# Hybrid attention layer on one core: the bias spread goes memory to memory, weight splits change engine, transposes go inside jobs, and keys are projected two heads at a time

## What is computed

```python
h = rmsnorm(x, g)                                   # 1040 x 1024
(c_q, c_kv, k_r, q_b, k_b, v_b, q_i, k_i, w_i, gate_a, gate_b) = split(h @ w_in)
q_a  = rmsnorm(c_q, g_cq) @ w_uq                    # 8 heads of 64 + 32
kv_a = (rmsnorm(c_kv, g_ckv) @ w_ukv).reshape(B, L, 8, 64 + 64)
k_nope, v_a = kv_a[..., :64], kv_a[..., 64:]
score = einsum('bqh,bqhk->bqk', w_i, relu(einsum('bqhd,bkd->bqhk', q_i, k_i)))
idx = top_k(score, 256)                             # keys of the sparse branch
bias = rel_bias[t5_bucket(idx - pos)]               # 32 buckets x 8 heads
```

## Time and profile before

| | |
|---|---|
| median of 3 runs | 1617.09 us (1616.66 to 1621.89) |
| the profiled execution's own time | 1617.06 us |
| its span | 1615.3 us |
| PE, DVE, ACT, POOL busy | 1400.2, 1035.6, 668.4, 438.2 us |
| index jobs, start of the first and last matmul | 28.0 and 99.9 us |
| first of the 64 steps | 137.2 us |
| first product for the keys of the first branch | 572.6 us |

### The profile page before, as it was taken

How to read it: one execution, slowest core, us unless ns; L and a number is a source line. 1 busy time by engine, 2 the same in 40 slices (tenths; PEclk the granted TensorE clock), 3 DMA queues, 4 the chain that set the end, 5 groups by cost and what they waited for, 6 DMA issues and landing times. The chain is left out here.

```text
span 1615.3 us, 21747 instructions
## 1 busy us (share of the span) xinstructions
PE 1400.2 (87%) x7342; PEld 1132.6 (70%) x7351; DVE 1035.6 (64%) x1946; ACT 668.4 (41%) x1179; POOL 438.2 (27%) x480
## 2 busy tenths in 40 slices
PE   5846999999999998989888988999945999999960
PEld 4645888878989757777666766889944777777730
DVE  4504899999990456666666665443264777777737
ACT  4305722322212146666665654111103666666622
POOL 2202044422212024434543411410002333333213
PEclk9877999999999999999999998999956999999985
DMA  7551031132223000203142205432164999999808
GB/s 205 57 69 40 24 137 53 46 98 82 89 92 110 23 0 5 69 1 99 47 93 60 54 1 190 145 99 79 66 261 147 344 355 356 357 372 376 327 31 324
DMA packets 86750, 217.36 MB, mean 135 GB/s; under 512 B 22712, under 2 KB 47832, under 8 KB 74376
## 3 DMA queue, kind: packets, MB, share of 16 engines
q1 hardware_dynamic: 76296, 195.24, 37.0%
q0 software_dynamic: 9216, 16.80, 2.8%
q10 hardware_dynamic: 1152, 4.19, 0.6%
HBM read 188.27 MB, written 44.70 MB: 144 GB/s over the span
## 5 line engine op out<-in xcount | busy, mean ns | idle before, releaser
L1269 DVE TENSOR_TENSOR pL<-ps,pH 128x512 fp32r<-128x512 f32 (+3 forms) x224 | 127.0, 574 | 113.2 <-ACT pH L1206 112.2
L416 PE MATMUL ps<-hHi,g_lead 128*128 128x512 f32 (+2 forms) x480 | 185.8, 387 | 9.1 <-DVE Qi L844 4.3
L310 DVE TENSOR_SCALAR_CACHE_REDUCE mask<-score,cand 128x272 bf16<-128x272 f32 (+6 forms) x224 | 185.5, 893 | 4.6 <-DVE cand L329 4.4
L417 PE MATMUL ps<-hLo,g_lead 128*128 128x512 f32 (+2 forms) x480 | 185.1, 386 | 0.0
L2178 DVE TENSOR_TENSOR w_rest<-wgu,w_lead 128x1024 fp32r<-128x1024 f32 x128 | 156.0, 1223 | 45.0 <-ACT w_lead L2125 43.8
L418 PE MATMUL ps<-hHi,g_rest 128*128 128x512 f32 (+2 forms) x480 | 184.0, 383 | 0.0
L732 POOL TENSOR_TENSOR g_rest<-g_raw,g_lead 128x2048 fp32r<-128x2048 f32 x16 | 73.6, 4601 | 320.4 <-ACT g_lead L591 320.4
L2125 ACT CAST w_lead<-wgu 128x1024 fp32r<-128x1024 f32 x128 | 134.4, 1055 | 37.9 <-PE ps L2071 37.9
L1206 ACT CAST pH<-ps 128x512 fp32r<-128x512 f32 (+3 forms) x224 | 108.1, 489 | 71.0 <-PE ps L1154 70.1
L2069 PE MATMUL ps<-w_lead,x_lead 128*128 128x512 f32 x256 | 114.1, 446 | 6.0 <-DVE w_rest L2178 6.0
L2091 PE MATMUL ps<-wd,hmT 128*128 128x512 f32 x256 | 115.3, 593 | 1.6 <-DVE hmT L2201 1.0
(11 more groups left out here) (348 smaller groups left out, 3466.3 us busy)
## 6 DMA issues: line engine op xcount, KB each, us to landing
wgu<-in_w_exp_gate SPq DMA_DIRECT2D x32, 1024.0 KB, 7.6
wgu<-in_w_exp_up SPq DMA_DIRECT2D x32, 1024.0 KB, 13.4
wd<-in_w_exp_down SPq DMA_DIRECT2D x32, 1024.0 KB, 13.8
g_raw<-in_w_in SPq DMA_DIRECT2D x16, 1024.0 KB, 5.8
gates_d<-stage SPq DMA_DIRECT2D x32, 256.0 KB, 2.0
gt<-gates_d SPq DMA_DIRECT2D x32, 256.0 KB, 3.2
rel_d<-relf SPq DMA_DIRECT2D x1, 4672.0 KB
KR<-kb_d SPq DMA_DIRECT2D x16, 260.0 KB, 6.4
```

Source lines behind the costliest of these rows:

```text
L310: return dve.tensor_scalar(mask[:, OFF[i]:OFF[i + 1]], score[:, OFF[i]:OFF[i + 1]], thr, 0.0, op, ALU.add, accum_out=cnt[:, i:i + 1])
L416: pe.matmul(dst, x[0], y[0], start=(k == 0), stop=False)
L417: pe.matmul(dst, x[0], y[1], start=False, stop=False)
L1269: dve.tensor_tensor(pL[n % RING][:, lo:512], bank_of(k)[:, lo:512], pH[n % RING][:, lo:512].bitcast(F32), ALU.subtract).then_inc(s_rs, 1)
```

## The change

- SP loads `rel_bias` and `hot` ahead of the first row block; PE makes the bias first, ahead of the row transposes. Row block 3 is loaded ahead of piece 0.
- ACT copies `relf` behind the first square, stores it to a new small `rel_s` (8 x 1168) in memory through its own queue, and behind the index jobs starts the spread from `rel_s` to `rel_d`, memory to memory.
- The remainders of pieces 0 to 3 are made by DVE, at other places of its stream; piece 4 and later stay on POOL. `lead(0)` moves one row block later, so does `lead(1)`; `lead(2)` comes behind all index outputs, `lead(3)` inside the steps.
- The transposes of row blocks 4 to 8 go inside the k loops of index jobs 0 to 2.
- `w_mla_ukv` is loaded as two tiles, `wuk` and `wuv`, with rows of 256 bytes; a key product covers two heads (12 products in place of 24), and both ACT and DVE copy out of each, one head each.

```diff
+        rel_s = dram("rel_s", (H, REL), F32)
-        kv_jobs = [("k", h, n) for h in range(H) for n in range(3)] + [("v", t, 0) for t in range(9)]
+        kv_jobs = [("k", h, n) for h in range(0, H, 2) for n in range(3)] + [("v", t, 0) for t in range(9)]
+
+        def copies(u, n):
+
+            return sum(kind == "k" or m % 2 == u for m, (kind, _, _) in enumerate(kv_jobs[:n + 1]))
...
+                sp.dma_start(rb32[:, :], a["rel_bias"]).then_inc(s_rel, 16)
+                sp.dma_start(hot[:, :], a["hot"]).then_inc(s_rel, 16)
                 rows_in(0)
...
                 rows_in(2)
+                rows_in(3)
                 piece_in(0)
-                rows_in(3)
-                sp.dma_start(rb32[:, :], a["rel_bias"]).then_inc(s_rel, 16)
-                sp.dma_start(hot[:, :], a["hot"]).then_inc(s_rel, 16)
...
-                sp.wait_ge(s_relc, 1)
-                sp.dma_start(rel_d, relf[:, :].unsqueeze(1).to_broadcast([H, P, REL])).then_inc(s_reld, 16)
...
-                            sp.dma_start(wukv[:, :], a["w_mla_ukv"][0]).then_inc(s_uw, 16)
+                            ukv = a["w_mla_ukv"][0].rearrange("c (h n) -> c h n", h=H)
+                            for k, w in enumerate((wuk, wuv)):
+                                sp.dma_start(w[:, :].rearrange("p (h n) -> p h n", h=H),
+                                             ukv[:, :, 64 * k:64 * (k + 1)]).then_inc(s_uw, 16)
...
                     for k in range(KT):
                         mm = three(ps[0:rows_out, 4 + n % 4, 0:hi - lo], (wl[:, k, c], wr_[:, k, c]),
                                    (hHi[:, k, lo:hi], hLo[:, k, lo:hi]), k)
-                    mm.then_inc(s_ij, 1)
+                        if k == KT - 1:
+                            mm.then_inc(s_ij, 1)
+                        if k in rows_between:
+                            transposes(rows_between[k])
...
                 for n in range(len(idx_jobs)):
-                    idx_job(n)
-                    if n < 4:
-                        transposes(4 + n)
-                    if n == 3:
-                        transposes(8)
+                    idx_job(n, {3: 4 + 2 * n, 7: 5 + 2 * n} if n < 2 else {3: 8} if n == 2 else {})
...
-                        if n % 2 == 0:
-                            pe.wait_ge(s_kva, n // 2 - 1)
-                        else:
-                            pe.wait_ge(s_kvd, n // 2 - 1)
+                        pe.wait_ge(s_kva, copies(0, n - 4))
+                        pe.wait_ge(s_kvd, copies(1, n - 4))
...
-                        mm = pe.matmul(bank[0:NOPE, 0:hi - lo], wk[:, i, 0:NOPE], ckvT[:, lo:hi],
+                        mm = pe.matmul(bank[:, 0:hi - lo], wuk[:, 64 * i:64 * (i + 2)], ckvT[:, lo:hi],
                                        start=True, stop=True)
...
+                    if b == 0:
                         act.wait_ge(s_relp, 3)
                         act.copy(relf[:, :], flat[0:H, 4 * 512:4 * 512 + REL]).then_inc(s_relc, 1)
-                    if b == 5:
+                        act.wait_ge(s_relc, 1)
+                        act.dma_start(rel_s, relf[:, :]).then_inc(s_rels, 16)
+                    else:
+                        rows_lead(b - 1)
+                    if b == 3:
+                        lead(0)
+                    if b == 6:
                         lead(1)
...
-                    if n == 7:
-                        lead(2)
-                    if n == 9:
-                        lead(3)
+                lead(2)
+                act.wait_ge(s_rels, 16)
+                act.dma_start(rel_d, rel_s.unsqueeze(1).to_broadcast([H, P, REL])).then_inc(s_reld, 16)
...
+                    if n == 12:
+                        lead(3)
...
-                    if b == 3:
-                        rest(0)
-                    if b == 6:
-                        rest(1)
...
-                for p in range(2, 5):
-                    rest(p)
+                rest(4)
...
+                def rest(p):
+                    dve.wait_ge(s_wh, p + 1)
+                    dve.tensor_tensor(g_rest[p % 2][:, :, :], g_raw[p % 2][:, :, :],
+                                      g_lead[p % 2][:, :, :].bitcast(F32), ALU.subtract).then_inc(s_wl, 1)
...
+                    if b == 7:
+                        rest(1)
                     if b >= 1:
                         rows_rest(b - 1)
+                    if b == 4:
+                        rest(0)
...
+                rest(2)
                 dve.wait_ge(s_wp, 4)
...
                     dve.wait_ge(s_re, n + 1)
+                    if n == 16:
+                        rest(3)
```

More of the change, by code:

```diff
@@ L226, in hybrid_layer @@
         wuq = at("wuq", [P, 2, H * QKD], F32, R_W)
-        wukv = at("wukv", [P, H * 128], F32, R_W + 6144)
+        wuk, wuv = (at(nm, [P, H * 64], F32, R_W + 6144 + off) for nm, off in (("wuk", 0), ("wuv", 2048)))
         qtok = [at(f"qtok{k}", [P, H, QKD], F32, R_W + 10240 + 3072 * k) for k in range(2)]
@@ L288, in step_at @@
             return (1024 * (n % 3) if n < WIDE else 1536 * (n % 2)) + chunks(WID[steps[n][0]])[0]
-        kv_jobs = [("k", h, n) for h in range(H) for n in range(3)] + [("v", t, 0) for t in range(9)]
+        kv_jobs = [("k", h, n) for h in range(0, H, 2) for n in range(3)] + [("v", t, 0) for t in range(9)]
+        def copies(u, n):
+            return sum(kind == "k" or m % 2 == u for m, (kind, _, _) in enumerate(kv_jobs[:n + 1]))
         (s_con, s_gain, s_gb, s_sq, s_nh, s_var, s_rstd, s_xn, s_tr, s_hh, s_hl, s_cb, s_rel, s_relp, s_relc,
-         s_reld) = map(sem, ["s_con", "s_gain", "s_gb", "s_sq", "s_nh", "s_var", "s_rstd", "s_xn", "s_tr", "s_hh",
-                             "s_hl", "s_cb", "s_rel", "s_relp", "s_relc", "s_reld"])
+         s_rels, s_reld) = map(sem, ["s_con", "s_gain", "s_gb", "s_sq", "s_nh", "s_var", "s_rstd", "s_xn", "s_tr", "s_hh",
+                             "s_hl", "s_cb", "s_rel", "s_relp", "s_relc", "s_rels", "s_reld"])
         s_xs = [sem(f"s_x{k}") for k in range(4)]
@@ L418, in three, with idx_job @@
                     return pe.matmul(dst, x[1], y[0], start=False, stop=(k == KT - 1))
-                def idx_job(n):
+                def idx_job(n, rows_between):
                     kind, p, t, part = idx_jobs[n]
@@ L478, in latent_rows @@
                     pe.transpose(ps[0:96, bank, 384:384 + r], krx[b % 2][0:r, :], ident[0:r, 0:r]).then_inc(s_gj, 1)
+                pe.wait_ge(s_rel, 32)
+                for c in range(0, REL, 512):
+                    n = min(512, REL - c)
+                    pe.matmul(flat[0:H, 4 * 512 + c:4 * 512 + c + n], rb32[:, :], hot[:, c:c + n],
+                              start=True, stop=True).then_inc(s_relp, 1)
                 pe.wait_ge(s_con, 16)
@@ L482, in _ @@
                     transposes(b)
[L483 to L489, removed]
-                for n in range(len(idx_jobs)):
-                    idx_job(n)
-                    if n < 4:
-                        transposes(4 + n)
-                    if n == 3:
-                        transposes(8)
+                for n in range(len(idx_jobs)):
+                    idx_job(n, {3: 4 + 2 * n, 7: 5 + 2 * n} if n < 2 else {3: 8} if n == 2 else {})
                 pe.wait_ge(s_il, 22)
@@ L535, in _ @@
                 pe.wait_ge(s_ge, NI)
-                pe.wait_ge(s_uw, 32)
+                pe.wait_ge(s_uw, 48)
                 for b in range(NB):
@@ L562, in _ @@
                         r = min(P, L - P * i)
-                        mm = pe.matmul(bank[0:r, :], ckvT[:, P * i:P * i + r], wk[:, :, NOPE:NOPE + VD],
+                        mm = pe.matmul(bank[0:r, :], ckvT[:, P * i:P * i + r], wuv[:, :],
                                        start=True, stop=True)
@@ L571, in q_out, with kv_copy @@
                                   ALU.mult).then_inc(s_qed, 1)
-            def kv_copy(eng, n, done):
+            def kv_copy(copy, u, n, done):
                 kind, i, part = kv_jobs[n]
-                eng.wait_ge(s_kv, n + 1)
                 bank = ps[:, 4 + n % 4, :]
-                copy = eng.copy if n % 2 == 0 else eng.tensor_copy
                 if kind == "k":
                     lo, hi = THIRD[part]
-                    copy(KTa[0:NOPE, i, lo:hi], bank[0:NOPE, 0:hi - lo]).then_inc(done, 1)
-                else:
+                    copy(KTa[0:NOPE, i + u, lo:hi], bank[NOPE * u:NOPE * (u + 1), 0:hi - lo]).then_inc(done, 1)
+                elif n % 2 == u:
                     r = min(P, L - P * i)
@@ L717, in _ @@
                     act.wait_ge(s_gds[k], 16 * len(range(k, len(jobs), 4)))
-                for n in range(0, len(kv_jobs), 2):
-                    kv_copy(act, n, s_kva)
-                    if n == 4:
+                for n in range(len(kv_jobs)):
+                    act.wait_ge(s_kv, n + 1)
+                    kv_copy(act.copy, 0, n, s_kva)
+                    if n == 2:
                         act.wait_ge(s_qea, NB)
```

(16 more changed lines are left out.)

5 lines of the change are left out of this document (removed).

## The result

The changed kernel takes 1573.99 us (median of 4, 1570.99 to 1575.06), against 1616.88 us of the kernel before beside it (median of 4): a ratio of 0.9728, 95% interval 0.9715 to 0.9742. Forecast were 1572.3 us and a range of 1564 to 1584.

What follows compares the result with a forecast made beforehand. The prediction took the slow bias spread, with piece 2 queued behind it, to bound the kernel. Its terms, −40.6 + 2.0 − 6.2 = −44.8 us on 1617.06, gave 1572.3 us, range 1564 to 1584.

Steps and rivals of the forecast that it cites:

- What bounds the kernel: Slow bias spread (51 GB/s) delays piece 2 behind it in SP's queue; no engine computes from 100 to 125 us.
- 1. The front: Row blocks ahead of the index jobs: job 0 starts at 28.8 us against 28.04, bounds 25 to 33.
- stated signs of being wrong: Among them, ahead of index jobs 0 to 2: gaps of PE beyond 3 us.
- 2. The index jobs: Index jobs on PE end at 91.9 us, against 100.0 before.
- 3. The hole: Between index jobs and steps: first gate matmul at 97.7 us, before 138.27; first three parts together give 40.6 us.
- 4. The steps: Gate steps: piece 3's cast and remainder move into them, 2 us lost, bounds 0 and 4.3.
- 5. The spread: Memory to memory from ACT's queue, from 96 us: 92 to 133 GB/s, done by 132 to 148, no cost.
- 6. The projections: Key products, twelve of 24 dropped: gain 6.2 us, bounds 3 and 7.
- the late collision: Rival: spread still at 51 GB/s runs 96 to 190, delays later loads; 18 us lost, 1590 us; chance 0.12.
- The front became a bound: Rival: each block costs DVE or ACT 1 us more; 5 to 7 us lost, 1578 us; chance 0.12.
- The products' rival, no gain: Rival: two copies in step bind the key products at over 1 us each; 1578 us; chance 0.04.
- Slower than before: Rival: spread at 36 GB/s or less starves PE of pieces; at 20 GB/s about 1700 us; chance 0.03.

Runs made afterwards that it cites:

- b1: Kernel before, with the bias stored to a small memory tensor and spread from there, at the old place on SP's queue: 1583.99 us, ratio 0.9791.
- b2: Kernel before, with the eight bias rows on partitions 0, 4, 8 to 28 instead of 0 to 7, spread from SBUF: 1583.74 us, ratio 0.9791.
- d1: Changed kernel with the spread put back: out of SBUF, on SP, ahead of pieces 2 and 3: 1604.24 us, ratio 0.9914.
- c3: Changed kernel, reordered: piece 0's remainder earlier on DVE, casts and remainders of pieces 2 and 3 inside or right behind last index jobs: 1563.11 us, ratio 0.9667.
- d2: Changed kernel with the spread's address order turned round, the 128 receiving partitions outermost: 1568.3 us, ratio 0.9708.
- a1: Changed kernel with the spread read from SBUF partitions 0 to 7 again, at its new place on ACT's queue: 1594.03 us, ratio 0.9848.
- c1: Changed kernel with 24 key products of one head each again, repeated beside the changed kernel: 1574.85 us, ratio 0.9744.

## Why the prediction was right, by its own steps

**What bounds the kernel.** Right, and shown from both sides: with only the spread mended (b1, b2) some 34 of the 43 us are there, and with all but that (d1) 30 to 34 are missing.

**1. The front.** Each of its rows was close: `hot` multiplied from 3.78 to 7.83 where 5.3 to 9.4 was expected, the square of block 4 ended at 21.71 against 23.1, job 0 at 27.52 against 28.8. ACT was through with the bias at 9.6, but its next block landed only at 10.53; that nothing else would wait for the queue was wrong by 1 us, without effect. What I had right for a reason that proved incomplete is that `rest(0)` sets job 0: it waits 5.66 us, and 2.6 of them were a matter of DVE's order (c3). By that wait one of the stated signs of being wrong did appear, a gap of PE beyond 3 us ahead of job 0; it was a badly chosen sign, since the forecast's own chain has PE idle there.

**2. The index jobs.** Forecast to end at 91.9, ended at 91.3. From 27.52 on PE has one gap, 0.75 us ahead of job 2, where I took 1.2 and 0.8 for the clock; job 2's matmuls stood 0.23 apart from the second on, so the gap cost no clock. The other way, twelve matmuls of job 0 stood 0.43 apart where I took nine.

**3. The hole.** Index weights at 93.97 (94.5), first gate matmul 97.15 (97.7): 41.1 us against 40.6.

**4. The steps.** The term was too large. I took 2 us lost; the steps' matmuls wait for `rt` twice, 0.30 and 0.59 us (once before, 0.2), and the stretch from the first gate matmul to the first key product lost 0.6. Only the 1.38 us ahead of the first gate matmul are a price of piece 2's late remainder, and that stood in part 3.

**5. The spread.** The price of nothing was right, the rate was not: I took half of what two loads reached, 92 to 133 GB/s; memory to memory on half of the engines gave 205. The step that failed is halving the loads' rate for half the engines: of d2's 300 to 320 the half-engine spread keeps two thirds, and already all of the smaller load's rate (184). What bound those two loads no run shows. The Trainium skill's figure, by which I had set an estimate of 22 us beside the sum (DMA: Bandwidth & Descriptors), was nearer the some 25 measured. It also was issued at 91.60 and moved from 93 on, not from 96 (below). Neither mattered, as up to 160 nothing large was to be met.

**6. The projections.** 6.35 us in the trace against 6.2, with one wait of 0.29 for DVE at the end; 6.3 in the times.

The sum was −44.8 against 43 of the medians and 46.1 of the spans. The parts gave 46.8 up to the next block, 2.0 more than forecast, and the medians 1.9 less; that the total came within 1.7 us of the median is partly luck, as the change's second runs, at 0.9705 or some 48 us of gain, say too. **The rivals:** the late collision is real, and what decided against it is the source in memory (a1). The front became a bound in a small way: c3 took 2.6 us out of it ahead of job 0, and 5.4 up to the first gate matmul. The products' rival, no gain, is refuted by c1. Slower than before was out of reach at 205 GB/s, and even a1, at 52, is some 25 us faster than before.

## What to carry to other kernels

A broadcast out of a few neighbouring partitions can hold a queue for 90 us while the engines show a share of only half: read the rate beside the share, and move the rows apart or through memory before moving the transfer. A transfer that no one awaits costs by what stands behind it and beside it, so another queue and a later place are only as good as the rate is. And when a long operation leaves an engine, place it by what stands behind it in the new stream: order alone gave 6 us in c3.

## What the runs showed of the hardware beyond the expected

- A transfer that ACT issues can start ahead of ACT's earlier work: in the changed kernel the issue at 91.60 stands in the stream behind `lead(2)`, which began at 92.87 and ended at 94.8, and the windows have the transfer moving from 93.1 on (109 GB/s from 93.1 to 93.4). The semaphore it waits for had long come.
- A broadcast from memory to memory moved 205 GB/s with half of the engines and 300 to 320 with all.
- After 5.66 us of idleness PE's first twelve index matmuls stood some 0.43 us apart, as others do from 97.75 on, where the windows give a granted clock of 0.50, the lower level. For job 0 the record of the clock says otherwise, so the slow start is read from the distances alone; the windows of the changed kernel:

```profile
28.00:32.00 4.00, 4.00 (x11) 3.05 (x10) 0.61 (x1) 0.00 (x0) 0.00 (x0) 1.00 0.00 0
95.00:100.00 5.00, 3.62 (x13) 2.92 (x13) 3.16 (x5) 1.26 (x4) 0.00 (x0) 0.50 0.50 184
```

  After 2.72 us, in c3, the first six did, and behind the seventh it was 0.35 and then 0.23. That it is the length of the gap that makes the difference wasn't tried by itself: in c3 the matmuls also begin earlier behind the transpositions.
